# Causal scores in four quadrants, and the order of their masked copies, in an RWKV-7 and sliding-window attention block

## What is computed

```
sa = einsum('bhvk,bhk->bhv', S, aa_t)
S = S * w_t[:, :, None, :] + sa[..., None] * bb_t[:, :, None, :] + v_t[..., None] * k_t[:, :, None, :]
y_t = einsum('bhvk,bhk->bhv', S, r_t)
```

## Time and profile before

| | |
|---|---|
| median of 3 runs | 1024.65 us (1024.53 to 1024.91) |
| the profiled execution, own time | 1024.74 us |
| span of its trace | 1023.0 us |
| VectorE, ScalarE, GpSimd busy | 72%, 51%, 22% |
| from one pair's scores to the next, pairs 3 to 6 | 40.6 us |
| pairs 1 and 2 | 40.9 us |

### The profile page before, as it was taken

One profiled execution on the slowest core, in us unless ns is written; L12 is line 12 of the kernel. 1 busy time (PEld: TensorE's weight loads), 2 busy tenths in 40 slices (PEclk: granted clock), 3 DMA queues, 4 the chain that ended last, 5 costly groups with the idle time before them and its releaser, 6 DMA issues.

```text
span 1023.0 us, 18730 instructions
## 1 busy us (share of the span) xinstructions
PE 1011.2 (99%) x7098; PEld 805.8 (79%) x7098; DVE 736.7 (72%) x1233; ACT 517.3 (51%) x869; POOL 224.4 (22%) x298
## 2 busy tenths in 40 slices
PE   8999999999999999999999999999999999999997
PEld 7888888777777777777777888888888888888886
DVE  5224666788988888888877565367777777789786
ACT  6435766844445445345453322265455444467744
POOL 8541356230321412314220554000000000000000
PEclk9999999999999999999999999999999999999999
DMA  7874465331303313214355867613333333336662
GB/s 201 240 223 135 130 218 197 91 78 42 87 24 74 87 63 86 57 62 119 95 163 151 239 232 257 202 36 103 88 103 89 97 101 103 90 116 223 206 186 116
DMA packets 161292, 133.25 MB, mean 130 GB/s; under 512 B 32730, under 2 KB 137736, under 8 KB 161224
## 3 DMA queue, kind: packets, MB, share of 16 engines
q1 hardware_dynamic: 147552, 88.37, 29.9%
q0 software_dynamic: 13520, 43.90, 13.9%
q10 hardware_dynamic: 151, 0.04, 0.0%
HBM read 111.83 MB, written 20.45 MB: 129 GB/s over the span
## 4 chain that ended last, share of the span: by engine, by line
PE 94%; DVE 2%; ACT 1%; issue 1%; DMA 1%; POOL 0%; ACTq 0%; DVEq 0%; POOLq 0%
PE ps L2082 15%; PE ps L2085 14%; PE ps L2084 14%; PE ps L2038 6%; PE ps L2040 5%; PE ps L2039 5%; PE ps L2640 3%; PE ps L2642 3%; PE ps L2641 3%; PE ps L2254 3%; PE ps L2388 2%; PE ps L2195 2%; PE ps L2576 1%; PE ps L2574 1%; PE ps L2575 1%; PE ps L2337 1%
## 5 line engine op out<-in xcount | busy, mean ns | idle before, releaser
L1351 DVE TENSOR_TENSOR wlo<-raw,whi 128x1024 fp32r<-128x1024 f32 x106 | 140.4, 1325 | 128.4 <-ACT whi L885 110.5
L885 ACT ACTIVATE whi<-raw 128x1024 fp32r<-128x1024 f32 x116 | 122.8, 1059 | 129.6 <-PE ps L2085 117.6
L2082 PE MATMUL ps<-xnh,whi 128*128 128x512 f32 x336 | 130.7, 389 | 0.0
L2084 PE MATMUL ps<-xnl,whi 128*128 128x512 f32 x336 | 130.7, 389 | 0.0
L2085 PE MATMUL ps<-xnh,wlo 128*128 128x512 f32 x336 | 130.7, 389 | 0.0
L2082 PE MATMUL ps<-xh,whi 128*128 128x512 f32 x232 | 91.5, 394 | 1.0 <-DVE xl L1369 1.0
L2084 PE MATMUL ps<-xl,whi 128*128 128x512 f32 x232 | 90.4, 390 | 0.0
L2085 PE MATMUL ps<-xh,wlo 128*128 128x512 f32 x232 | 90.3, 389 | 0.0
L2038 PE MATMUL ps<-xh,whi 128*128 128x512 f32 x192 | 89.5, 466 | 0.0
L2040 PE MATMUL ps<-xh,wlo 128*128 128x512 f32 x192 | 76.1, 396 | 0.0
L2039 PE MATMUL ps<-xl,whi 128*128 128x512 f32 x192 | 75.3, 392 | 0.0
(11 more groups left out here) (425 smaller groups left out, 2441.0 us busy)
## 6 DMA issues: line engine op xcount, KB each, us to landing
raw<-in_w_in SPq DMA_DIRECT2D x108, 256.0 KB, 3.2
raw<-in_w_up SPq DMA_DIRECT2D x88, 256.0 KB, 3.0
wrow<-in_w_down POOLq DMA_DIRECT2D x22, 512.0 KB, 4.7
raw<-weight_scratch SPq DMA_DIRECT2D x44, 256.0 KB, 3.4
raw<-in_w_down SPq DMA_DIRECT2D x32, 256.0 KB, 2.9
weight_scratch<-wrow POOLq DMA_DIRECT2D x11, 512.0 KB, 3.4
gates_scratch<-gst POOLq DMA_DIRECT2D x16, 256.0 KB, 3.3
raw<-in_w_proj_b SPq DMA_DIRECT2D x16, 256.0 KB, 4.1
```

The lines of the kernel that those rows point to most:

```text
L885: act.activation(flat(whi[:, hb]), flat(raw[:, b]), ACT.Copy).then_inc(w_hi, 1)
L1351: dve.tensor_tensor(flat(lo[:, hb]), flat(raw[:, b]), flat(hi[:, hb]).bitcast(F32), ALU.subtract).then_inc(w_lo, 1)
L2082: pe.matmul(ps[bank][:, :], whi[:, hb, k, :], hi(k), start=first and k == 0, stop=False)
L2084: pe.matmul(ps[bank][:, :], whi[:, hb, k, :], lo(k), start=False, stop=False)
```

## The change

Scores are made only where the mask can keep something. Of a chunk's 128 x 128 square, the queries 0 to 63 can see only the keys 0 to 63 (the early quadrant), the queries 64 to 127 see all keys (the late half). Early: 16 matmuls of 64 rows, 64 output rows and 128 moving columns (64 of a~, 64 of r~), chunk `j` = 2 jj + e into partitions e x 64 on of bank 2 or 3 (by head). Late: 16 matmuls of 64 rows, 128 output rows and 128 moving columns into banks 0, 1 (`bp`) and 4, 5 (`kp`). The masked copies are again eight of 512 elements per partition: four early ones, on 64 partitions each, which fill both gb and gk (now one tile `gg`), and four late ones on 128 partitions. The early ones wait for all early matmuls, and in pair 0 for `cleared` at 2. DVE's new order is the four early copies, the two late ones of gb, `value_tokens`, the two late ones of gk, `invert`; `deviations` of the pair before goes behind the level-0 masks. `score_copy` waits for six copies instead of four. On PE `turned_var` moves behind the transposes of bp, and `deviations` from between bp's transposes and the "centred" fill to behind L2314 of level 1. The transposes of z wait for two copies, of bp for four, of kp for six (before: three, four, eight).

```diff
-SCORE_BANK = (0, 1, 2, 3, 4, 5, 0, 1)
+EARLY_BANK = (2, 3)
+LATE_BANK = ((0, 1), (4, 5))
...
-        gb = take("gb", [P, NT, 2, 2 * C])
+        gg = take("gg", [P, NT, 2, 2, 2, C])
+        gb, gk = (gg[:, 2 * i:2 * i + 2].rearrange("p x e h q t -> p (x e) h (q t)")
+                  for i in range(2))
...
             def score_copy(n):
-                act.wait_ge(g_ready, n * 8 + 4)
+                act.wait_ge(g_ready, n * 8 + 6)
...
+            def predicated(dst, mask, scores, f):
+                dve.memset(carrier[:, f:f + 1], 0.0)
+                dve.copy_predicated(dst, mask.bitcast(U32).unsqueeze(1)
+                                    .to_broadcast([mask.shape[0], NT, 2, C // 2]), scores)\
+                    .then_inc(g_ready, 1)
+
+            def late_masked(n, i, h):
+                f = 4 + 2 * i + h
                 if n == 0:
-                    dve.wait_ge(cleared, 1 + f // 4)
+                    dve.wait_ge(cleared, 1 + i)
                 dve.wait_ge(g_ps, n * 8 + f + 1)
+                predicated((gb, gk)[i][:, :, h, :].rearrange("p j (q t) -> p j q t", q=2)
+                           [:, :, :, C // 2:], two_parts(causal[:, :], slice(C // 2, C)),
+                           ps[LATE_BANK[i][h]][:, :].rearrange("p (j q t) -> p j q t", j=NT, q=2), f)
+
+            def early_masked(n, h, e):
+                if n == 0:
+                    dve.wait_ge(cleared, 2)
+                dve.wait_ge(g_ps, n * 8 + 4)
+                predicated(gg[0:HD, :, e, h, :, 0:C // 2],
+                           two_parts(causal[0:HD, :], slice(0, C // 2)),
+                           ps[EARLY_BANK[h]][e * HD:(e + 1) * HD, :]
+                           .rearrange("p (x q t) -> p x q t", x=NT, q=2), 2 * h + e)
...
+                    if lv == 0 and d is not None:
+                        deviations(d)
...
-                for f in range(6):
-                    masked(n, f)
-                deviations(n - 1)
-                for f in range(6, 8):
-                    masked(n, f)
+                masked(n, 0)
                 value_tokens(n)
+                masked(n, 1)
...
+                for i, src in enumerate((bp, kp)):
+                    for jj in range(2):
+                        o = (2 * i + jj) * C
+                        for e in range(2):
+                            j = 2 * jj + e
+                            for h, hs in enumerate(rows):
+                                ins = pe.matmul(ps[EARLY_BANK[h]][e * HD:(e + 1) * HD, o:o + C]
+                                                .rearrange("p (q t) -> p q t", q=2),
+                                                src[hs, j * C:j * C + HD], both(hs, j, slice(0, HD)),
+                                                start=True, stop=True)
+                                if i and jj:
+                                    ins.then_inc(g_ps, 1)
+                late(0)
+                late(1)
                 if d is not None:
                     norm_var(d)
                 fill("scores")
-                if d is not None:
-                    turned_var(d)
-                pe.wait_ge(g_ready, n * 8 + 3)
+                pe.wait_ge(g_ready, n * 8 + 2)
                 turned(2, z[:, n + 16, :]).then_inc(tok_ps, 1)
                 pe.wait_ge(g_ready, n * 8 + 4)
                 turned(3, bp).then_inc(tok_ps, 1)
                 if d is not None:
-                    deviations(d)
+                    turned_var(d)
                 fill("centred")
-                pe.wait_ge(g_ready, n * 8 + 8)
+                pe.wait_ge(g_ready, n * 8 + 6)
                 turned(1, kp).then_inc(tok_ps, 1)
...
+                    if lv == 1 and d is not None:
+                        deviations(d)
                     fill((lv, "masks"))
```

More of the change, by code:

```diff
@@ L278, in build @@
         ysb = take("ysb", [P, T])
-        gk = take("gk", [P, NT, 2, 2 * C])
         rkcols = take("rkcols", [P, P // NT])
@@ L1513, in deviations, with two_parts, masked @@
                 spread(ysq, ystd).then_inc(vex_ready, 1)
-            def masked(n, f):
-                j0, h = (f % 4) // 2 * 2, f % 2
-                dst = (gb, gk)[f // 4][:, j0:j0 + 2, h, :]
+            def two_parts(t, ts):
+                return t.rearrange("p (q t) -> p q t", q=2)[:, :, ts]
+            def predicated(dst, mask, scores, f):
[5 more added lines that the diff above has]
+                f = 4 + 2 * i + h
                 if n == 0:
-                    dve.wait_ge(cleared, 1 + f // 4)
+                    dve.wait_ge(cleared, 1 + i)
                 dve.wait_ge(g_ps, n * 8 + f + 1)
[L1523 to L1527, removed]
+                predicated((gb, gk)[i][:, :, h, :].rearrange("p j (q t) -> p j q t", q=2)
[9 more added lines that the diff above has]
+                           .rearrange("p (x q t) -> p x q t", x=NT, q=2), 2 * h + e)
+            def masked(n, i):
+                if i == 0:
+                    for h in range(2):
+                        for e in range(2):
+                            early_masked(n, h, e)
+                for h in range(2):
+                    late_masked(n, i, h)
             def add_bonus(d):
@@ L1708, in _ @@
             weights(n + 2)
-            for f in range(8):
-                masked(0, f)
+            masked(0, 0)
             value_tokens(0)
+            masked(0, 1)
             invert(0, None, True)
@@ L2246, in scores, with both, late @@
                     pe.wait_ge(ps_free, N_FILL - 1)
[L2247 to L2256, removed]
+                rows = [slice(h * HD, (h + 1) * HD) for h in range(2)]
+                def both(hs, j, ts):
+                    return ar[hs, 1 - n % 2, j, :].rearrange("p (q t) -> p q t", q=2)[:, :, ts]
+                def late(i):
+                    src = (bp, kp)[i]
+                    for j in range(NT):
+                        for h, hs in enumerate(rows):
+                            ins = pe.matmul(ps[LATE_BANK[i][h]][:, j * C:(j + 1) * C]
+                                            .rearrange("p (q t) -> p q t", q=2),
+                                            src[hs, j * C:(j + 1) * C], both(hs, j, slice(HD, C)),
                                             start=True, stop=True)
-                            if j > j0:
+                            if j == NT - 1:
                                 ins.then_inc(g_ps, 1)
+                for i, src in enumerate((bp, kp)):
+                    for jj in range(2):
+                        o = (2 * i + jj) * C
+                        for e in range(2):
+                            j = 2 * jj + e
+                            for h, hs in enumerate(rows):
+                                ins = pe.matmul(ps[EARLY_BANK[h]][e * HD:(e + 1) * HD, o:o + C]
+                                                .rearrange("p (q t) -> p q t", q=2),
+                                                src[hs, j * C:j * C + HD], both(hs, j, slice(0, HD)),
[4 more added lines that the diff above has]
+                late(1)
                 if d is not None:
```

## The result

The changed kernel took 1031.47 us (median of 6 runs, 1030.84 to 1031.81) against 1024.88 for the kernel before (6 runs, 1024.53 to 1025.06): ratio 1.0063, interval 1.0053 to 1.0074. It is slower by 6.6 us; the forecast was 1026.0, and the range ended at 1029. The profiled execution took 1031.70 with a span of 1030.0.

The account below looks back on a forecast made before the run. The prediction took TensorE, busy 99% of the span, to bound the kernel. Terms of -0.40, -0.06 and +1.75 summed to +1.3 us on the profiled 1024.74, so 1026.0 us, with a range of 1020.0 to 1029.0.

Parts of the forecast that it names:

- Change 1: Score matmuls: early quadrants run four at once, so scores take 2.95 us instead of 3.66, 0.71 less.
- Rival (b): Early score quadrants run only two at a time, first copy at 2.05: +7.1, 1031.9 us; chance 0.13.
- Change 2: TensorE's own waits: 0.12 us before the kp transposes goes; TensorE does 0.8 less but waits for masks and spread.
- Change 3: Chain behind the copies: sixth copy at 4.30, update at 11.45 against 11.53, 0.08 us saved per regular pair.
- Rival (c): Masked copies are dearer in runs of 64 elements, 0.045 us each: +2.2, 1028.2 us; chance 0.09.
- the hold of `xx` by `remainder`: VectorE's `xx` waits in every pair until POOL's `remainder` ends at 8.36, so the masks start at 8.85.
- rival (a): No hold of `xx` by `remainder`, masks at 8.18: -4.1, 1020.7 us; chance 0.18.
- Change 4: Pair 0: early copies wait for gk's clearing, first copy at 218.02 instead of 216.08; +1.75 us.
- Sum: Whole kernel: -0.40 for pairs 3 to 7, -0.06 for pairs 1 and 2, +1.75 for pair 0, giving +1.3 us.

Follow-up runs that it names:

- experiment 1: The changed kernel with its four early masked copies reordered, both heads of the lower output partitions first, then both of the upper; 1028.96 us, ratio 1.0040 to the kernel before.
- experiments 4: The changed kernel with GpSimd's `remainder` told to wait for VectorE's `xx` as well; 1037.83 us, ratio 1.0124 to the kernel before.
- experiment 6: The changed kernel with experiment 1's copy order, `remainder` behind `xx` and the spread, and the bonus rows' round trip ahead of it; 1023.78 us, ratio 0.9992 to the kernel before.

## Why the prediction was wrong

**Change 1, right.** Four quadrants at once, 3.02 to the variances instead of 2.95. Rival (b) is out, though its 1031.9 lies nearest to the measured time: it priced a late chain, and another cause made the chain late.

**Change 2, right in kind.** TensorE does less and waits for the chain in every pair.

**Change 3, here the forecast failed**, at one step: "Six starts took 462.60 - 459.42 = 3.18, so the sixth copy [...] starts at 4.30". It took the distance of 0.64 over from copies that all start at partition 0. That half the partitions are no cheaper was right; that they could be dearer by their order had no term. The sixth copy started at 5.00. Rival (c) had the right place, at 0.045 a copy, and the wrong cause, the short runs: copies with runs of 64 elements stand 0.63 apart in experiment 1. The distance isn't set by the copy's size but by where its score input starts: 0.77 where the start moves between 0 and 64, 0.63 to 0.65 where it doesn't (experiment 1). Four of the five distances ahead of n1 were long: 4 x 0.14 = 0.56. The first copy was another 0.14 late (1.26 instead of 1.12); its cause wasn't tried. Together 0.70, and the update was 0.66 late. The Trainium skill, "VectorE: DVE Perf Modes", section "Two Vector instructions with no wait between them", has this rule, as a model: an instruction is held when an input starts at another partition quadrant than that of the last one that read the same memory, and the held one begins only when the earlier ones have finished. The trace agrees: the copy of 466.04 ends at 466.78 and the next starts at 466.81, while in experiment 1 the second starts 0.10 ahead of the first one's end. The prediction weighed the tiles of the array and the shared ports, not this.

The rest of this step held: the hold of `xx` by `remainder` in each pair (rival (a) is out, as experiments 4 and 6 show by lifting it), n1, masks and spread at the forecast distances. From it alone the seven pairs behind pair 0 would have saved 0.46; with seven times 0.66 they would lose 4.2; the spans show 3.9.

**Change 4, right in mechanism, too small.** The first copy of pair 0 was at 3.56 for 3.54. Missing were the held copies (0.5, the same term) and the fall of TensorE's clock behind its waits (0.6): +2.95 instead of +1.75. The step took TensorE to be "1.75 later", as if its idle time left its pace alone. The reading ahead of it, a clock that is "full in all 40 slices", was already a little too strong: a 9 stands for 90% or more, and in the kernel before the granted clock is 0.50 in the window 1022 to 1024 us.

**Sum.** +1.3 forecast, 7 x 0.66 = 4.6 from the copies' chain, 0.5 + 0.6 in pair 0: together +7.0, and the two spans differ by 7.0. That it closes so well is in part luck: by stages pair 0 has 2.95 where these terms give 2.85, the rest 3.93 for 4.16, and the scores begin 0.12 later. The range's upper end, 1029, came from rival (c)'s price; a cost per copy bounded by the nearest rows didn't cover a mechanism that none of these rows contained, since before every copy had its input at partition 0.

## What to carry to other kernels

When a full-height VectorE instruction is cut into parts, order the parts so that consecutive ones read from the same start partition. When VectorE work is moved earlier, look up which POOL instruction it will then lie beside; a hold that is lifted in one place appears at the next instruction of the same kind, so move the POOL instruction behind the last of them. Work taken from the engine that bounds the kernel is worth nothing if the chain beside it has no slack, and every idle stretch that it opens can cost TensorE its clock as well.

## What the runs showed of the hardware that was not expected

- A change of the start partition between two VectorE copies from PSUM costs 0.14 us (0.77 against 0.63), with 512 elements per partition each.
- A POOL instruction holds not only a VectorE instruction with two SBUF inputs (`xx`, 0.68 to 1.36) but also a plain f32 copy within SBUF (the spread, 0.43 to 1.75) and a TENSOR_SCALAR (0.49 to 2.17, one record, beside a POOL MEMSET, which reads nothing). Each ended 0.27 to 0.55 behind POOL. The masks, with one input in PSUM, were not held. The Trainium skill, "SBUF — State Buffer", section "Who interferes with whom", separates these cases in the same way: two SBUF inputs contend with a GpSimd instruction that reads SBUF, `copy` and `tensor_scalar` can take the shared ports in a two-port mode, and at most one SBUF input outside such a mode is free. Which mode an instruction ran in no trace here shows.
- In pair 0 TensorE's granted clock was 0.50 behind idle stretches of 1.11 and 0.87 us in the changed kernel, and 1.00 in experiment 1, whose copies there were 0.28 faster. That isn't the copies' doing alone: experiment 6 has the same order, the same idle stretch of 1.73, and 0.50 in that window; its pair 0 took 42.72 against 42.32. So the fall is worth about 0.4 to 0.6, and whether it comes near these idle lengths changes from execution to execution. Of the changed kernel's six runs four have a mean granted clock of 0.997 (1031.22 to 1031.81) and two of 1.0 (1030.84 and 1031.25).
